# Streaming a closing RMS norm inside the last expert group of a decoder layer

## What is computed

```python
def moe_ffn(h, ...):                      # top 4 of 32 experts per token
    xs = hf[tok]                          # rows sorted by expert
    gate, up = jnp.split(lax.ragged_dot(xs, w_gu, group_sizes) + b_gu[sorted_e], 2, axis=-1)
    gate = jnp.minimum(gate, 7.0); up = jnp.clip(up, -7.0, 7.0)
    act = (up + 1.0) * (gate * jax.nn.sigmoid(1.702 * gate))
    out = (lax.ragged_dot(act, w_down, group_sizes) + b_down[sorted_e]) * weights
    return zeros.at[tok].add(out)
x = x + g2 * moe_ffn(...)
return rmsnorm(x, norm_f)                 # x * rsqrt(mean(x * x) + 1e-6) * norm_f
```

## Time and profile before

| | us |
|---|---|
| median of 3 runs | 4118.63 (4117.14 to 4118.73) |
| the profiled execution | 4121.83 |
| its span, first to last instruction | 4120.1 |
| PE busy | 3904.0 (95%) |
| DVE, ACT, POOL busy | 2352.0, 1530.1, 567.1 |
| DMA, moved in all | 763 MB, 185 GB/s on average |

### The profile page before, as it was taken

One profiled execution on the slowest core, in us unless ns is written; L12 is line 12 of the kernel. 1 busy time (PEld: TensorE's weight loads), 2 busy tenths in 40 slices (PEclk: granted clock), 3 DMA queues, 4 the chain that ended last, 5 costly groups with the idle time before them and its releaser, 6 DMA issues. The chain is left out here.

```text
span 4120.1 us, 64304 instructions
## 1 busy us (share of the span) xinstructions
PE 3904.0 (95%) x18356; PEld 3205.4 (78%) x18357; DVE 2352.0 (57%) x3725; ACT 1530.1 (37%) x2258; POOL 567.1 (14%) x600
## 2 busy tenths in 40 slices
PE   7999999898979999999999999999999999999993
PEld 4888788787868878878778888878888788888782
DVE  5263342795765764554675666586565656444742
ACT  3222321662223542342453444364343434322532
POOL 1110110111221111101110201111110211111102
PEclk9999999899989999999999999999999999999997
DMA  6442441764345774565684777597575856544826
GB/s 240 156 133 87 156 142 57 251 208 153 133 143 186 244 266 122 153 221 137 201 280 165 222 241 229 151 344 226 167 222 177 258 166 220 163 122 114 268 96 188
DMA packets 347524, 763.09 MB, mean 185 GB/s; under 512 B 29849, under 2 KB 29906, under 8 KB 342818
## 3 DMA queue, kind: packets, MB, share of 16 engines
q1 hardware_dynamic: 289138, 600.04, 42.3%
q0 software_dynamic: 55120, 151.68, 15.0%
q10 hardware_dynamic: 3200, 10.53, 0.6%
HBM read 653.81 MB, written 108.33 MB: 185 GB/s over the span
## 5 line engine op out<-in xcount | busy, mean ns | idle before, releaser
L1860 ACT CAST weights_split<-weights_raw 128x1024 fp32r<-128x1024 f32 x420 | 431.4, 1054 | 536.3 <-PE tok_bank_acc L118 487.2
L116 PE MATMUL tok_bank_acc<-weights_first,weights_split 128*128 128x512 f32 x1264 | 506.2, 401 | 11.4 <-DVE weights_first L1953 9.3
L1953 DVE TENSOR_TENSOR weights_split<-weights_raw,weights_split 128x1024 fp32r<-128x1024 f32 x420 | 490.7, 1220 | 22.0 <-ACT weights_split L1860 13.0
L116 PE MATMUL tok_bank_acc<-weights_split 128*128 128x512 f32 x1264 | 498.4, 394 | 0.8 <-DVE weights_split L1953 0.8
L1953 DVE TENSOR_TENSOR weights_first<-weights_raw,weights_first 128x1024 fp32r<-128x1024 f32 x416 | 483.8, 1219 | 20.7 <-ACT weights_first L1860 18.8
L117 PE MATMUL tok_bank_acc<-weights_split 128*128 128x512 f32 x1264 | 495.6, 392 | 0.0
L118 PE MATMUL tok_bank_acc<-weights_split 128*128 128x512 f32 x1264 | 495.4, 392 | 0.0
L118 PE MATMUL tok_bank_acc<-weights_first,weights_split 128*128 128x512 f32 x1264 | 494.3, 391 | 0.0
L117 PE MATMUL tok_bank_acc<-weights_first,weights_split 128*128 128x512 f32 x1264 | 493.7, 391 | 0.0
L1838 POOL DMA_INDIRECT y_rows<-tok_act_row,tok_token x123 | 199.6, 1622 | 2130.3 <-DVE tok_act_row L2022 2080.7
L1860 ACT CAST weights_first<-weights_raw 128x1024 fp32r<-128x1024 f32 x416 | 425.5, 1050 | 168.8 <-PE tok_bank_acc L118 125.9
(11 more groups left out here) (327 smaller groups left out, 6594.1 us busy)
## 6 DMA issues: line engine op xcount, KB each, us to landing
weights_raw<-in_w_gu SPq DMA_DIRECT2D x560, 512.0 KB
weights_raw<-in_w_down SPq DMA_DIRECT2D x280, 512.0 KB
tok_bias<-in_b_gu SPq DMA_DIRECT2D x35, 1024.0 KB
early_w_raw<-in_w_in POOLq DMA_DIRECT2D x14, 2048.0 KB, 11.1
proj<-pro_stage SPq DMA_DIRECT2D x112, 256.0 KB, 2.0
pro_w_ada<-in_w_ada POOLq DMA_DIRECT2D x64, 256.0 KB, 3.5
mix_late<-proj SPq DMA_DIRECT2D x48, 256.0 KB, 3.7
mod_w_ada<-in_w_ada SPq DMA_DIRECT2D x8, 1024.0 KB, 16.0
```

The source lines that it names most:

```text
L116: nc.tensor.matmul(out, act_hi, w_hi, start=first, stop=False)
L1860: nc.scalar.copy(whi[c % 2][:, j * SK:(j + 1) * SK], raw[:, n % RAW]).then_inc(hi_done, 1)
L1953: nc.vector.tensor_tensor(wlo[c % 2][:, rows], raw[:, n % RAW], whi[c % 2][:, rows], ALU.subtract).then_inc(lo_done, 1)
```

## The change

`phase_finish` is removed. Its work is written into the group loop of `expert_programs`, in branches that are taken in the last group alone (`nT < 1`).

- SP, in the last group, behind its weight loads: reads `norm_f` over the routing records in `rec`, and tiles 0 to 7 of `y` into the eight `raw` slots as these come free; then it writes each scaled tile, and after the four writes of a set have landed reads the tiles that follow in its slots. The four sets have four tiles each.
- ScalarE: set 0 is squared behind the cast of tile 1's second activations, its roots taken in one instruction behind that of tile 2, followed by one small Silu. Sets 1 to 3 are squared and rooted behind the loop's last casts, then the last group's own rows, then one small Silu. Squares are written to the PSUM bank `tx`.
- VectorE: set 0 is scaled ahead of the weighing of chunk 4, tile 3. Behind chunk 4 it adds the earlier rows to the weighed results in `xs`, scales sets 1 and 2, then weighs chunk 5 with the addition, scales set 3, and scales the last group's own rows.
- POOL: in the last group it doesn't add to `y`, but gathers the earlier rows of the group's tokens into `xs`. Behind the group loop it waits for all tile writes, then writes the last group's rows over them with indirect writes, up to one for each tile.
- The weighing of chunk 5 stands twice now, once under `nT > 0` and once in the last group's branch.

TensorE's program is not changed. The core of the diff:

```diff
@@ sync(sp), in the group
+                with sp.If(G.nT < 1):
+                    sp.wait_ge(token_set, g + 1)
...
+                    sp.wait_ge(share_set, g + 1)
+                    sp.dma_start(norm_f, A["norm_f"].partition_broadcast(P)).then_inc(nf_in, 16)
+                    for half in range(2):
+                        sp.wait_ge(y_out[half], G.landed(0))
...
+                    for i in range(RAW):
+                        sp.wait_ge(lo_done, G.pieces(PIECES * NCH - RAW + i + 1))
+                        load_tile(i)
+                    for b, tiles in enumerate(SETS):
+                        for i in tiles:
+                            sp.wait_ge(z_done, i + 1)
+                            sp.dma_start(out_t[:, i], whole(i)).then_inc(fin_out[b], 16)
+                        again = [i + RAW for i in tiles if i + RAW < NT]
+                        if again:
+                            sp.wait_ge(fin_out[b], 16 * len(tiles))
+                        for i in again:
+                            load_tile(i)
@@ gpsimd(pool)
+                with pool.If(G.nT < 1):
+                    pool.wait_ge(tx_done, G.before + G.T + 1)
...
+                    for t in range(GT):
+                        with pool.If(G.T > t):
+                            for half in range(2):
+                                pool.indirect_dma_start(
+                                    out=xs[:, t, half * N:(half + 1) * N], out_offset=None, in_=keep["y"][half],
+                                    in_offset=bass.IndirectOffsetOnAxis(ap=token[:, t:t + 1], axis=0)
+                                    ).then_inc(prior_in, 16)
...
-        for half in range(2):
-            pool.wait_ge(y_out[half], total * 16 + 16)
+        for b, tiles in enumerate(SETS):
+            pool.wait_ge(fin_out[b], 16 * len(tiles))
+        T = last_tiles(pool)
+        for t in range(GT):
+            with pool.If(T > t):
+                pool.wait_ge(last_row, t + 1)
+                pool.indirect_dma_start(
+                    out=out_rows, out_offset=bass.IndirectOffsetOnAxis(ap=token[:, t:t + 1], axis=0),
+                    in_=xs[:, t], in_offset=None, bounds_check=S - 1, oob_is_err=False).then_inc(row_out, 16)
+        pool.wait_ge(row_out, T * 16)
@@ scalar(act), in the group
                 for t in range(1, GT):
                     with act.If(G.T > t):
                         activations_hi(1, t)
+                        if t == 1:
+                            with act.If(nT < 1):
+                                set_squared(0)
+                        if t == 2:
+                            with act.If(nT < 1):
+                                set_rms(0)
+                                gate_table()
...
+                with act.If(nT < 1):
+                    with act.If(G.T < 2):
+                        set_squared(0)
+                    with act.If(G.T < 3):
+                        set_rms(0)
+                    for b in range(1, len(SETS)):
+                        set_squared(b)
+                        set_rms(b)
+                    for t in range(GT):
+                        with act.If(G.T > t):
+                            act.wait_ge(sum_done, G.T + (t + 1))
+                            mean_square(xs[:, t], NT + t, last_sq, t + 1)
+                            root(slice(NT + t, NT + t + 1), last_rms)
+                    gate_table()
@@ vector(dve), in the group
                         activations_lo(1, t)
+                        if t == GT - 1:
+                            with dve.If(nT < 1):
+                                set_out(0)
                         weigh(NGU, t)
...
+                with dve.If(nT < 1):
+                    dve.wait_ge(prior_in, G.T * 32)
...
+                    for t in range(GT):
+                        with dve.If(G.T > t):
+                            add_prior(NGU, t)
+                    with dve.If(G.T < GT):
+                        set_out(0)
+                    set_out(1)
+                    set_out(2)
+                    for t in range(GT):
+                        with dve.If(G.T > t):
+                            weigh(NGU + 1, t, last=True)
+                            add_prior(NGU + 1, t)
+                    set_out(3)
+                    for t in range(GT):
+                        with dve.If(G.T > t):
+                            last_rows_out(t)
```

More of the change, by code:

```diff
@@ L1696, in expert_programs, with whole, last_tiles @@
     rows_left, LEFT = keep["rows_left"], 5
+    (nf_in, sq_done, rms_done, inv_done, z_done, prior_in, sum_done, last_sq, last_rms, last_inv, last_row,
+     row_out) = k.sems("nf_in sq_done rms_done inv_done z_done prior_in sum_done last_sq last_rms last_inv last_row row_out")
+    BATCH = 4
+    SETS = [range(b, b + BATCH) for b in range(0, NT, BATCH)]
+    fin_in = [k.sem(f"fin_in{b}") for b in range(len(SETS))]
+    fin_out = [k.sem(f"fin_out{b}") for b in range(len(SETS))]
+    of_set = {i: b for b, tiles in enumerate(SETS) for i in tiles}
+    y_t = [a.rearrange("(t p) n -> p t n", p=P) for a in keep["y"]]
+    out_t = keep["out"].rearrange("o (t p) d -> p (o t) d", p=P)
+    out_rows = keep["out"].rearrange("o s d -> (o s) d")
+    norm_f = rec[:].bitcast(F32).rearrange("p q c -> p (q c)")
+    junk = tx[:].rearrange("p a b c -> p (a b c)")
+    def whole(i):
+        return raw[:, i % RAW].rearrange("p s n -> p (s n)")
+    def last_tiles(eng):
+        groups = eng.value_load(table[0:1, COUNT:COUNT + 1], min_val=1, max_val=NG)
+        return tiles_in(load_word(eng, groups - 1))
     y_out = [y_out0, y_out1]
@@ L2018, in weigh @@
                         dve.wait_ge(y_out[1], G.landed(0))
-                    if c == NGU + 1 and t == 1:
+                    if c == NGU + 1 and t == 1 and not last:
                         dve.wait_ge(y_out[0], G.landed(G.T))
@@ L2063, in vector @@
                         weights_lo(g + 1, n)
-                for t in range(GT):
-                    with dve.If(G.T > t):
-                        weigh(NGU + 1, t)
+                    for t in range(GT):
+                        with dve.If(G.T > t):
+                            weigh(NGU + 1, t)
+                with dve.If(nT < 1):
+                    dve.wait_ge(prior_in, G.T * 32)
+                    dve.sem_inc(wait_carrier, 1)
+                    for t in range(GT):
[10 more added lines that the diff above has]
+                    set_out(3)
+                    for t in range(GT):
+                        with dve.If(G.T > t):
+                            last_rows_out(t)
                 dve.nop()
@@ L2296, in program @@
             run(phase_tokens)
-        run(phase_finish)
 _INS = ['x', 'c', 'positions', 'w_ada', 'b_ada', 'norm1', 'w_in', 'w_gk2', 'b_gk', 'gla_onorm', 'ret_onorm', 'w_out',
```

111 lines of the change are left out of this document (54 added, 57 removed).

## The result

The changed kernel took **4268.66 us** (median of 4 runs, 4265.08 to 4272.21); the kernel before, run beside it, took 4118.68 us (4117.14 to 4122.49). The ratio is 1.036, 95% interval 1.035 to 1.038: it is 150 us slower, where 4082 us and a gain of 37 us were forecast. The profiled execution took 4265.08 us, span 4263.3.

A forecast was written before the change was run, and what follows sets the result against it. TensorE was taken as the bound, leaving its 65.2 us idle end to win. Ending at 4081.9 plus 1.5 for groups gave a 4083.4 span; less 1.5 for the median, 4082 us (-37); range 4075 to 4092.

The forecast's parts named there:

- rival C: Group loop: longer bodies leave the instruction buffers and are fetched each pass; 4162 us; chance 0.06 in full, 0.03 in part.
- What every group pays: Group loop, each pass: skipped branches at 0.3 us matter only in ten one-tile groups, 0 to 3 us, taken as 1.5.
- an unlucky place: VectorE's loop body: a condition, beside a miscount of 120 instructions, under which a body of 390 would not fit 512.
- The empty passes, which jump over the body in 0.3 us, agree: VectorE's 12 empty passes at the loop's end: their short jumps taken as support that the body stays in the buffer.
- C's price: Group loop: four fetches a pass at 2.0 us, 8 us in each of ten one-tile groups, 80 us; others hide most.
- The mechanism of the tail: Behind the last matmul: weigh-and-add pairs, set 3, last rows, row writes and both engines' ends, from 4054.85 to 4081.9.
- A set's reads: Set 2 in the last group: eight loads take 3.8 us to issue, the last lands about 4 us later, at 4045.5.
- So VectorE is not kept: Behind the last matmul: set 3's squares and root ready at 4061.6, before VectorE finishes its weigh-and-add pairs at 4061.7.
- rival B: Sets 2 and 3: the slots' serial write and read round trips bound the end; 4088 to 4103 us, chance 0.12.
- The first row write: GpSimd behind the loop: tile writes issued by 4067.1 land 2.9 us later at 4070; first row write at 4070.5.
- The end: VectorE's tail ends at 4080.1, GpSimd's at 4080.2 to 4081.1 including its DRAIN; 1.2 us for barrier and clearing gives 4081.9.
- Set 0 at no cost: Last group: set 0's squares, root and scalings fit in gaps of ScalarE and VectorE; nobody waits, cost nothing.

The follow-up runs named there:

- dve_behind: Changed kernel with VectorE's last part written behind the group loop instead of in it, loop body 288 instructions; 4091.02 us.
- hybrid: dve_behind with VectorE's first additions and set 1 back in the loop, body moved 74 instructions later, GpSimd reading its tile count before its waits; 4084.58 us.
- after_shift40: Changed kernel with a never entered block ahead of VectorE's group loop, moving its 366-instruction body 39 instructions later; 4087.29 us.
- no_out1: after_shift40 without the writes of tiles 4 to 7 and the wait for their slots; 4087.59 us in one run.
- The padded kernel with 30: Kernel before the change with 30 never-run VectorE instructions at the end of its loop body, 313 in all; 4292.12 us.

## Why the prediction was wrong, step by step

**The step that failed: rival C was given 0.06 because a body of some 390 "still fits".** It took a buffer's capacity for the length of loop that it keeps. In the sum this is the term "What every group pays": 1.5 us for skipped branches and nothing for fetches, where the loop grew by 176.1 us. The case shows that 366 instructions are refetched in each pass at one place and not at another, and 313 too. The 512 instructions of the Trainium skill (Runtime: NRT & Kernel Launch, Instruction fetch mechanics) are not what decides here: at the old place the limit lay between 288 and 313. The prediction had "an unlucky place" as a condition, but no way to price it: the trace of before shows only that 281 fitted at 1309, and that says nothing of 366. A step from 281 to 366 with no row between should have had a chance nearer to even than to one in ten, and the range should have reached C's 4162, which would still have fallen 107 us short.

**"The empty passes, which jump over the body in 0.3 us, agree"** was no evidence: they jump over a body of 281 that the buffer held. In after the same 12 passes take longer: from the last scaling to VectorE's DRAIN 4261.93 - 4250.06 = 11.9 us instead of 8.95. Nearly all of the difference is the first of them: between the loop's branch at 4250.1 and the next record of the head, at 4253.0, there is none. The others follow at 0.76 us, by these records of the head from 4250 us on:

```profile
L2113 DVEq COMPARE_BRANCH  x13: 50/56/72, 4250.1 to 4261.8; - x13
L2113 DVEq MOVE  x12: 36/36/36, 4253.0 to 4261.4; - x12
```

**C's price: "in a one-tile group 8 us ... the other groups would hide most".** The number per one-tile group was too high: it measured 5.7 and 4.5 us in the two of the earlier trace rows, where they went from 36.8 to 42.5 and from 39.2 to 43.7, and 4.3 on average of ten. Five packets came where four were supposed, so one cost less than the 2.0 us that was taken for it. What failed is that the others would hide it: they hid little. The argument was VectorE's busy share, 58.93 of 141.50 us in the last group; but four of the five fetches come within 9 us of the turn between passes (the windows of q14 above), when TensorE waits for the first low parts of the new rows and weights, and there VectorE has no slack in a group of any size, as the lengths by number of tiles show. 35 x 5.0 = 176 us instead of 10 x 8 = 80. And it did not allow for the clock: +47 us of the 176 are the same matmuls running longer, after idle stretches that the kernel before did not have.

**What every group pays for branches: +1.5 us.** With the fetches away, the loop takes 2827.5 (dve_behind) and 2825.0 (hybrid) against 2826.2. That agrees, but 1.5 us is too small to be read from runs that differ by several. In after_shift40's profiled execution it takes 2833.8, but that one was the slowest of its four runs.

**The mechanism of the tail was right, 6.5 us too short.** TensorE's last product to the end of the span: forecast 4081.9 - 4054.85 = 27.05, measured 33.5 in after. Its rows on VectorE, behind the last product:

```profile
4226.84 0.18 DVE L2124 RECIPROCAL tok_bias<-tok_bias 128x4 f32<-128x4 f32 x1 [9.92 <-ACT tok_bias L1969]
4227.06 4.87 DVE L2128 SCALAR_TENSOR_TENSOR weights_raw<-weights_raw,tok_bias,tok_rec 128x1024 f32<-128x1024 f32 x4
4231.85 0.75 DVE L2160 SCALAR_TENSOR_TENSOR tok_gate_up<-tok_bank_acc,tok_share,tok_g 128x512 f32<-128x512 f32 x1
...
4240.68 0.18 DVE L2124 RECIPROCAL tok_bias<-tok_bias 128x4 f32<-128x4 f32 x1 [3.20 <-ACT tok_bias L1969]
...
4250.06 1.28 DVE L2128 SCALAR_TENSOR_TENSOR tok_rows<-tok_rows,tok_bias,tok_rec 128x1024 f32<-128x1024 f32 x1
```

Set by set: one set 4.9 to 5.0 us with its reciprocal (forecast 5.0); the four pairs 4231.85 to 4237.5, 5.6 (5.9); the four last rows 1.39 each (1.45). What was mis-sized:
- A set's reads. SP issues those of set 2 from 4212.27 and ScalarE's first square of it starts at 4221.78: 9.5 us, where 8 was taken.
- "So VectorE is not kept" for set 3. It waits 3.20 us: rival B's mechanism in small, as no_out1 shows. In time from the last product, set 3's reads are issued 2.8 us later than forecast (4226.75, 3.0 us ahead of the product's end, against 4049 and 5.8), and the first square stands 8.9 us behind that issue where 7.5 was taken. Together the last scaling starts 20.3 us behind the last product, not 16.3: +4.0.
- The first row write. It goes out at 4251.03, 4.9 us after SP's last issue (4230.47 + 15.66), where 3.4 was taken (4067.1 to 4070.5). The landing was priced right: GpSimd's wait ends at 4248.7, 2.6 us after the issue (2.9 taken). The rest is GpSimd reading the tile count only then, its first load at 4248.8, and setting up the write. In hybrid, which reads the count ahead of the wait, the wait ends at 4070.0 and the first row write starts at 4071.05.
- The end. After the row writes, 1.3 apart as priced, GpSimd's DRAIN takes 2.64 us (1.4 to 2.3 was taken).
- VectorE's DRAIN, 2.9 us later than from 8.95, by the stall in the first empty pass. In after this tail was last, by half a microsecond; with the body held, GpSimd's is.

SP's issues in the timeline of after, the end of GpSimd's wait and its first load of the count, and its row writes:

```profile
4212.27 3.66 SPq L1821 DMA_DIRECT2D weights_raw<-y_rows  x8
...
4230.47 15.66 SPq L1829 DMA_DIRECT2D out<-weights_raw  x8
```

```profile
L1905 POOLq EVENT_SEMAPHORE  x2: 17/30/43, 4240.6 to 4248.7; - x2
...
L1718 POOLq TENSOR_LOAD <-tok_table x1: 302/302/302, 4248.8 to 4248.8; - x1
```

```profile
4251.03 1.20 POOL L1910 DMA_INDIRECT out<-tok_rows,tok_token  x1 [136.10 <-issue]
4252.53 1.00 POOL L1910 DMA_INDIRECT out<-tok_rows,tok_token  x1 [0.30 <-issue]
```

Without the fetches these sizes are nearly all that is left of the error: after_shift40 and hybrid, at 4087.29 and 4084.58 us, lie 5 and 3 us above the 4082 forecast and inside its range of 4075 to 4092.

**Set 0 at no cost** was right: its four scalings start 0.2 us behind the reciprocal at 4203.78 and nobody waits for the weighing behind them at 4208.77. A second table load, at 4203.26 ahead of set 1's squares, was not foreseen and cost nothing: VectorE doesn't wait for set 1.

## What to carry to other kernels

A loop body that grows on one engine is a change to that engine's instruction supply, whatever the added instructions do and even if they never run. Look at the instruction queue of the engine (here q14, 29 packets or 202) before and after, and at waits by "issue" at the head of a pass; if packets come with every pass, put code that runs once behind the loop, or move the loop some tens of instructions, and measure at more than one place. Code behind the loop pays for passes that the input leaves empty, here 10.2 us. And ask of a stall that is added to every pass not how busy the engine is in the pass, but whether somebody waits for it at the spot where the stall falls.

## What was not expected of the hardware

- Whether VectorE's loop body is fetched again in each pass depends on where it lies: 366 instructions cost 176 us over 35 passes with the head at 1309 and nothing at 1348.
- In length it is a cliff: 313 and 366 instructions at the same head both bring five packets of 8.2 KB a pass, and 4292 and 4299 us.
- The same five packets cost 5.0 us a pass at one place and 3.3 at another, for a reason that was not tested.
- TensorE's granted clock went from 0.99 to 0.97 over the loop and from 1.00 to 0.96 in the first one-tile group, once it stood idle at the head of each pass: its matmuls there were busy for 47 us more. The padded kernel with 30, which has none of the change's work, shows the same rise (2798.5 us busy, 0.98).
